# A second feed-forward computed by block products: gate, up and down in pairs of tiles

## The reference, cut to what matters

```python
D_MODEL, D_FF, SEQ, MACARON_WEIGHT = 1024, 2816, 512, 0.5

def swiglu(h, w_gate, w_up, w_down):
    return (jax.nn.silu(h @ w_gate) * (h @ w_up)) @ w_down

def ffn_sublayer(t, shift, scale, gate, norm_g, w_gate, w_up, w_down):
    h = modulate(rms_norm(t, norm_g), shift, scale)
    return t + gate * (MACARON_WEIGHT * swiglu(h, w_gate, w_up, w_down))
```

## Time and profile before

| what | us |
|---|---|
| median of 3 executions | 1463.39 (1462.80 to 1463.84) |
| profiled execution, first to last instruction | 1459.6 |
| TensorE busy in it | 1429.1 (98%) |
| VectorE / ScalarE / GpSimd busy | 705.8 / 265.9 / 664.1 |
| second feed-forward behind its first segment, on TensorE | 1150.2 to 1446.9 |

### The profile page before, as it was taken

One profiled execution on the slowest core, in us unless ns is written; L12 is line 12 of the kernel. 1 busy time (PEld: TensorE's weight loads), 2 busy tenths in 40 slices (PEclk: granted clock), 3 DMA queues, 4 the chain that ended last, 5 costly groups with the idle time before them and its releaser, 6 DMA issues.

```text
span 1459.6 us, 19101 instructions
## 1 busy us (share of the span) xinstructions
PE 1429.1 (98%) x7912; PEld 1250.1 (86%) x7912; DVE 705.8 (48%) x1032; ACT 265.9 (18%) x440; POOL 664.1 (46%) x389
## 2 busy tenths in 40 slices
PE   7999999999999999999999999999999999999997
PEld 3699999999999999987898888888898888888886
DVE  2774467467454554246636449625775112112114
ACT  3320010010010010023634321124131000000104
POOL 1363443433433433433610456624738557566661
PEclk9999999999999999999999999999999999999999
DMA  9532353353343343114310278384646323233321
GB/s 350 159 109 63 117 147 117 104 146 104 117 129 121 117 122 116 44 38 125 88 30 1 59 193 224 103 258 155 204 134 187 101 87 101 87 101 101 95 65 58
DMA packets 232563, 174.31 MB, mean 119 GB/s; under 512 B 28664, under 2 KB 212124, under 8 KB 232476
## 3 DMA queue, kind: packets, MB, share of 16 engines
q1 hardware_dynamic: 213296, 142.50, 33.4%
q10 hardware_dynamic: 19180, 30.58, 6.5%
HBM read 155.26 MB, written 17.79 MB: 119 GB/s over the span
## 4 chain that ended last, share of the span: by engine, by line
PE 93%; DVE 3%; ACT 1%; issue 1%; DMA 1%; POOL 0%; SPq 0%; DVEq 0%; POOLq 0%; ACTq 0%
PE ps L888 59%; PE ps L1143 15%; PE ps L1146 4%; PE ps L897 2%; PE ps L920 2%; PE ps L1240 2%; PE ps L1095 1%; PE ps L985 1%; PE ps L976 1%; PE ps L1393 1%; PE ps L1050 1%; PE ps L1347 1%; PE ps L1351 1%; PE ps L1162 1%; DMA x_in<-in_ctx_dram 1%
## 5 line engine op out<-in xcount | busy, mean ns | idle before, releaser
L818 POOL TENSOR_SCALAR w_hi<-w_raw 128x1024 fp32r<-128x1024 f32 (+1 forms) x187 | 211.6, 1131 | 745.2 <-issue 458.4
L821 POOL TENSOR_TENSOR w_lo<-w_raw,w_hi 128x1024 fp32r<-128x1024 f32 (+1 forms) x187 | 451.1, 2413 | 15.6
L888 PE MATMUL ps<-h_hi,w_lo 128*128 128x384 f32 (+1 forms) x1224 | 381.4, 360 | 0.0
L888 PE MATMUL ps<-h_hi,w_hi 128*128 128x384 f32 (+1 forms) x1224 | 378.6, 358 | 0.0
L888 PE MATMUL ps<-h_lo,w_hi 128*128 128x384 f32 (+1 forms) x1224 | 378.4, 358 | 0.0
L888 PEld LDWEIGHTS ps<-h_hi,w_lo 128*128 128x128 f32 x1224 | 221.9, 189 | 23.7 <-issue 2.5
L888 PEld LDWEIGHTS ps<-h_hi,w_hi 128*128 128x128 f32 x1224 | 223.9, 189 | 20.4
L888 PEld LDWEIGHTS ps<-h_lo,w_hi 128*128 128x128 f32 x1224 | 223.7, 189 | 20.4
L2196 DVE SCALAR_TENSOR_TENSOR ps<-ps,silu 128x768 f32<-128x768 f32 (+1 forms) x44 | 36.5, 831 | 254.6 <-PE ps L888 248.4
L2226 DVE SCALAR_TENSOR_TENSOR x<-ps,mod,x 128x512 f32<-128x512 f32 x88 | 64.8, 750 | 168.8 <-PE ps L1146 91.4
L1143 PE MATMUL ps<-act_hi,w_lo 128*128 128x512 f32 x336 | 133.7, 398 | 1.8 <-DVEq L2201 1.8
(11 more groups left out here) (374 smaller groups left out, 1868.4 us busy)
## 6 DMA issues: line engine op xcount, KB each, us to landing
w_raw<-in_ffn_w_gate_dram SPq DMA_DIRECT2D x44, 512.0 KB, 3.9
w_raw<-in_ffn_w_up_dram SPq DMA_DIRECT2D x44, 512.0 KB, 3.9
w_raw<-in_ffn_w_down_dram SPq DMA_DIRECT2D x40, 512.0 KB, 3.6
ada_w<-in_ada_w_dram ACTq DMA_DIRECT2D x32, 512.0 KB, 4.3
w_raw<-in_w_in_dram SPq DMA_DIRECT2D x32, 512.0 KB, 4.1
ada_w<-in_ada_w_dram SPq DMA_DIRECT2D x30, 512.0 KB, 4.8
c_scr<-cp ACTq DMA_DIRECT2D x16, 288.0 KB, 4.1
b_scr<-bt_sb ACTq DMA_DIRECT2D x16, 256.0 KB, 3.9
```

The source lines that it names most:

```text
L818: pool.tensor_scalar(w_hi[:, s, 0:cols], w_raw[:, s, 0:cols], 1.0, 1.0, ALU.mult, ALU.mult)\
L821: pool.tensor_tensor(w_lo[:, s, 0:cols], w_raw[:, s, 0:cols], w_hi[:, s, 0:cols].bitcast(F32), ALU.subtract).then_inc(w_split, 1)
L888: last = pe.matmul(mv[2], st, mv[part], start=(first and q == 0), stop=(n == len(terms) - 1 and q == 2))
```

## The change

The first segment stays. The other 18 hidden tiles are taken as nine pairs. Gate of a pair is a 1024x256 by 1024x512 product. It is cut into 2x2 blocks of weights and 2x2 blocks of `h`, and computed by Winograd's form of Strassen's scheme: seven block products in place of eight, each 4 x 3 matmuls of 256 columns. Up of the pair likewise. A "group" is the gate or the up of one pair. The order of stages is written out in `STAGES`: group 0, group 1, then for each pair the gate group, the down projection of the pair before, the up group; the last two down projections end it. So there are seven gate groups with a down projection behind them (groups 2, 4, ..., 14).

- **Sums of h** (`tiles_of_h`, `copy_h`, `tile_hi`): four sums of blocks of `h`, built once in the first segment in the odd PSUM banks, VectorE 28 operations of 128x512, ScalarE 12 copies. Each stands behind the ada additions of a hidden tile. TensorE waits for the first two (`t_ok`) before `ada_sums`.
- **Sums of weights** (`weight_sums`): four additions or subtractions of 128x512 on VectorE for each group, one operand or the result in PSUM banks 3 and 7, with block A21 first copied to bank 3 by ScalarE (`copy_a21`).
- **High and low parts**: high parts move from GpSimd to ScalarE (`prepare`), in blocks of 128x512 through eight half slots, seven blocks ahead (`LEAD`). GpSimd makes the low parts, but VectorE those of the two sums that lie in PSUM (`low_ahead`).
- **Partial products**: ScalarE copies three partial results of a group out of PSUM (`part`), VectorE adds them to later products in three additions of 128x256 (`quarter_ok`), then come SiLU, product, high copy and low part by quarters of 128x256.
- **Loads**: both units of a stage are loaded when GpSimd has made the low part of the last block of the stage two before (for a down stage, of its blocks one by one).
- **Semaphores**: two are gone, and the gate loads share those of the first ada tiles.

Its core, with the order of the queues:

```diff
@@ constants
+PAIRS = (FF // P - SEG) // 2
+HT = NL // 2
+HK = KD // 2
+PRODUCTS = ("p1", "p7", "p6", "p4", "p5", "p2", "p3")
+RAW_BLOCK = {"p1": (0, 0), "p4": (1, 1), "p2": (0, 1)}
+SUMS_FOR = {"p7": 1, "p6": 4, "p5": 4, "p3": 4}
+BY_DVE = ("p6", "p5")
+LEAD = 7
+STAGES = [("group", 0), ("group", 1)]
+for _m in range(1, PAIRS - 1):
+    STAGES += [("group", 2 * _m), ("down", _m - 1), ("group", 2 * _m + 1)]
+STAGES += [("group", 2 * PAIRS - 2), ("group", 2 * PAIRS - 1), ("down", PAIRS - 2), ("down", PAIRS - 1)]
@@ sync
+            def raw_read(st, v):
+                if st < 2:
+                    sp.wait_ge(w_split, PAIR_UNIT0 + 2 * st + v + 1)
+                elif STAGES[st - 2][0] == "group":
+                    pool_low_made(sp, BLOCK0[st - 2] + NPROD - 1)
+                else:
+                    pool_low_made(sp, BLOCK0[st - 2] + 2 * v + 1)
@@ tensor
                         if not two and nth == 0 and v == 2 * tiles - 1:
+                            pe.wait_ge(t_ok, 4)
                             pe.wait_ge(acc_ok, ada_added(ADA_MIX + 1, KD))
...
+            def group(q):
...
+                block_product(q, 0, "a", True, False)
...
+                block_product(q, 1, "b", True, False)
+                pe.wait_ge(part_ok, 3 * q + 1)
+                block_product(q, 2, "a", False, False)
+                pe.wait_ge(part_ok, 3 * q + 2)
+                block_product(q, 3, "b", False, True)
+                pe.wait_ge(part_ok, 3 * q + 3)
+                block_product(q, 4, "a", False, False)
...
+                block_product(q, 5, "c", True, True)
+                pe.wait_ge(quarter_ok, 3 * q + 2)
+                block_product(q, 6, "a", False, True)
@@ scalar
+            def copy_a21(q):
+                raw_here(act, stage_unit("group", q) + 1)
...
+                act.activation(ps[:, 3, :], raw_block(q, 1, 0), ACT.Copy).then_inc(a21_copied, 1)
+            def prepare(b):
...
+                if b + 2 in GROUP_AT:
+                    copy_a21(GROUP_AT[b + 2])
+            def group(q):
...
+                b = block_of("group", q, 0) + LEAD
+                for i in range(3):
+                    part(i, "aba"[i])
+                    prepare(b + i)
+                prepare(b + 3)
+                prepare(b + 4)
+                quarter(0)
+                prepare(b + 5)
+                quarter(1)
+                prepare(b + 6)
+                quarter(2)
+                quarter(3)
@@ vector
+            def weight_sums(q):
...
+                for f in range(2):
+                    raw_here(dve, stage_unit("group", q) + f)
+                dve.wait_ge(a21_copied, q + 1)
...
+                TT(s3, a11, a21, ALU.subtract).then_inc(sum_ok, 1)
+                TT(s1, a21, a22, ALU.add).then_inc(sum_ok, 1)
+                dve.wait_ge(sum_ok, 4 * q + 2)
+                TT(s2, s1, a11, ALU.subtract).then_inc(sum_ok, 1)
+                dve.wait_ge(sum_ok, 4 * q + 3)
+                TT(s4, a12, s2, ALU.subtract).then_inc(sum_ok, 1)
+            def st_group(q):
...
+                def event(i):
+                    b = block_of("group", q, i)
+                    sums_ahead(b + LEAD)
+                    low_ahead(b + LEAD - 1)
+                for i in range(3):
+                    event(i)
+                product_done(dve, q, 3)
+                dve.wait_ge(part_ok, 3 * q + 3)
+                TT(bank_b, bank_b, s2, ALU.add).then_inc(quarter_ok, 1)
+                event(3)
+                product_done(dve, q, 4)
...
+                TT(last_quarter(q), bank_a, s7, ALU.add).then_inc(quarter_ok, 1)
+                event(4)
+                if up:
+                    gated(0)
+                    gated(1)
+                product_done(dve, q, 5)
+                TT(bank_c, bank_c, s1, ALU.add).then_inc(quarter_ok, 1)
...
@@ vector, first segment, behind the ada additions of tile f_
+                            tiles_of_h(f_)
```

More of the change, by code:

```diff
@@ new lines, in bank_read @@
+            def bank_read(q, name):
+                if q < 2:
+                    for j in range(down_job(0, 0) - 4, down_job(0, 0)):
+                        if 2 * (j % 4) == 4 * q + "abc".index(name):
+                            was_read(pe, j)
+                    return
+                m = q // 2 - 1 - (q % 2 == 0 or q == GROUPS - 1)
+                for e, bank in enumerate(DOWN_BANKS[m] if m >= 0 else ()):
+                    if bank == 4 * (q % 2) + "abc".index(name) and bank not in DOWN_BANKS[m][e + 1:]:
+                        was_read(pe, down_job(m, e))
@@ L1499, in _ @@
+            for kind, n in STAGES:
+                (group if kind == "group" else down)(n)
             for k in range(4):
@@ L1624, in ada_tile, with ffn @@
                 act.dma_start(ada_w[:, s, :], ada_src(g, k)).then_inc(ada_here[s], 16)
-            def ffn(jobs, parts, n, act_base):
+            def ffn(jobs, parts, n, act_base, blocks_of_h=None):
                 def seg(part, i):
@@ L1922, in _, with copy_h, tile_hi @@
                 hi_half(1, k)
-            ffn(JOB["ffn2"], PARTS2, NL, FF // P)
+            def copy_h(n):
+                act.wait_ge(hb_ok, KD)
+                for b in range(2):
+                    act.activation(odd_bank(1 - n, b), two(h_hi[:, HK * n:HK * n + HK, HT:2 * HT], b).bitcast(F32), ACT.Copy)                        .then_inc(h_copied, 1)
+            def tile_hi(t):
+                for b in range(2):
+                    act.wait_ge(t_made, 2 * t + b + 1)
+                    act.activation(two(t_hi(T_ORDER[t]), b), odd_bank(T_BANKS[t], b), ACT.Copy).then_inc(t_hi_ok, 1)
@@ L1924, in _ @@
+            copy_a21(0)
+            for b in range(LEAD):
+                prepare(b)
+            for kind, n in STAGES:
+                if kind == "group":
+                    group(n)
+                else:
+                    for i in range(4):
+                        prepare(block_of("down", n, i) + LEAD)
             norm(3, JOB["norm3"], NL)
@@ new lines, in st_down @@
+            def st_down(m):
+                for e in range(KD):
+                    j = down_job(m, e)
+                    is_done(dve, j)
+                    STT(x[:, e, 0:NL], ps[:, DOWN_BANKS[m][e], :], mod[:, 64 + e, 0:1], x[:, e, 0:NL], ALU.mult, ALU.add)\
+                        .then_inc(slot_read[j % 4], 1)
+                    if m == PAIRS - 1 and e:
+                        add_square(3, e - 1, NL)
+                    if e % 2:
+                        b = block_of("down", m, e // 2)
+                        sums_ahead(b + LEAD)
+                        low_ahead(b + LEAD - 1)
+                if m == PAIRS - 1:
+                    add_square(3, KD - 1, NL)
+                was_read(dve, down_job(m, KD - 1))
@@ L2232, in seg @@
                             ada_add(ADA_START + nth, KD - 1)
+                        if q and k == 3:
+                            weight_sums(0)
+                        if q and k == 6:
+                            low_ahead(block_of("group", 0, 2))
                         if tiles == TAIL and k:
@@ L2716, in _ @@
             ffn(JOB["ffn2"], PARTS2, NL, 2, FF // P)
+            low_ahead(block_of("group", 0, 4))
+            weight_sums(1)
+            for kind, n in STAGES:
+                (st_group if kind == "group" else st_down)(n)
             was_read(dve, JOB["norm3"])
```

300 lines of the change are left out of this document (291 added, 9 removed).

## The result

| kernel | median us | executions | ratio to the kernel before |
|---|---|---|---|
| before, beside it | 1463.10 | 1461.41 to 1463.84 | |
| changed | 1483.16 | 1482.83 to 1488.62 | 1.0149 [1.0131, 1.0167] |
| changed, timed a second time | 1487.02 | 1485.74 to 1489.69 | 1.0156 [1.0143, 1.0170] |

What follows compares the result with a forecast made beforehand. The prediction took TensorE, busy for 98% of the span, as the bound. Its terms -14.4 - 2.8 + 7.2 + 19.6 = +9.6 us took the median 1463.39 to 1473.0 us, range 1453 to 1486.

Steps and rivals of the forecast that it cites:

- Part 1: Gate and up of the 18 later tiles: 1512 narrow matmuls in place of 864 wide ones, gain 14.4 us.
- Part 2: Five VectorE detours at segment ends go, as the down projection now runs one pair behind: gain 2.8 us.
- Part 3: First segment: VectorE's h sums delay TensorE, 5 us before the ada sums, 2 in the fourth down job; loss 7.2 us.
- Part 4: Seven gate groups before a down projection: TensorE waits 2.8 us each before the seventh product, loss 19.6 us.
- Edits costed at nothing: Partial-product copies, high and low parts, other groups' weight sums, and removed semaphores: no added time.
- The rival of the other side: Queues hide more: VectorE gets weight tiles early, h sums fit its idle time; 1458 or 1446 us; chance 0.24.

Runs made afterwards that it cites:

- filled waits: Changed kernel with TensorE making the sixth product three times over in the seven gate groups before a down projection; 1479.98 us, against 1487.02 unfilled beside it.
- short h sums: Changed kernel with the 20 additions and subtractions for the sums of h run over 8 of 256 columns per block; 1479.94 us, one execution.
- Short weight sums: Changed kernel with the weight sums of the groups from the third on run over 16 of 512 columns, order untouched; 1465.67 us, one execution.
- sums moved behind the addition: Changed kernel, with VectorE's four weight sums behind the addition for product 5 in the seven gate groups before a down projection; 1459.30 us, ratio 0.9965.
- both orders mended: Changed kernel with weight sums behind product 5's addition, second SiLU quarter earlier in those gate groups, and most h sums later in the first segment; 1451.67 us, ratio 0.9919.

## Why the prediction was wrong in size

The forecast's four parts, with what the runs showed:

| part | forecast | measured |
|---|---|---|
| 1. narrow matmuls | -14.4 | -14.4 (0.120 us apart, as said) |
| 2. waits at the ends of segments | -2.8 | -2.8 (no wait ahead of a down projection) |
| 3. first segment | +7.2 | +5.1 of waits |
| 4. seven gate groups | +19.6 | +22.7 (20.9 of waits, 1.8 of restarts) |
| TensorE at 1.2 GHz behind the waits | not in the sum | +11.2 (4.0 and 7.2) |
| sum | +9.6 | +21.8 (spans: +21.5) |

- **The step that failed** is in parts 3 and 4: each wait was costed at its own length, and TensorE was taken to go on at 0.2267 and 0.120 us a matmul behind it. In its place, the clock fell behind six of the eight waits, and the slow matmuls took 11.2 us more. Of the 4.0 in the first segment some 2.6 stand where TensorE would have waited for VectorE anyway (the slot at 1138.3, above), so about 1.4 + 7.2 = 8.6 us are net. They are most of the 12.2 us by which the sum was off; 3.1 are part 4's longer waits and restarts, 0.5 the rest of part 3. The filled waits show the pair part's share as an effect of the idle time, not of the work around it.
- **The trace of before had it.** The rows that the forecast rests on do not show it: TensorE's clock reads 1.00 through the earlier trace rows, where no wait is longer than 0.3 us. Elsewhere the same trace does. Behind a wait of 2.76 us at 53.46 the clock reads 0.58, and from 401.85 it reads 0.57 with no wait at all; ahead of that stand 32 matmuls of one column and 8 of 128 columns (397.32 to 401.9):

```profile
53.46:57.46 4.00, 4.00 (x14) 4.00 (x15) 4.00 (x9) 4.00 (x9) 0.00 (x0) 0.58 0.00 0
401.85:405.85 4.00, 4.00 (x15) 4.00 (x15) 2.87 (x5) 0.81 (x1) 2.70 (x2) 0.57 0.00 0
```

- **Part 1** held. The 109.2 ns that the forecast gives from the Trainium skill ("TensorE: Matmul & The Clock Gate", Back-to-back issue gap) did not show: neighbouring starts in the block products lie 0.12 us apart.
- **Part 2** held: the list of waits has none in front of the down projections of the pairs.
- **Part 3**, the first wait, was right (5 forecast, 5.83 measured), and the short h sums show that it is theirs. The second, 2 us in the fourth down job, did not show, because slow matmuls stood in its place: VectorE's low part came within 0.5 us of the forecast, but TensorE came later still. By the slot alone the loss would have been 7.7 us (9.1 less 1.4, an estimate), beside the 7.2 of the forecast. So VectorE's queue was worked out rightly. The 5.1 in the table is smaller because slow matmuls filled part of that time.
- **Part 4**, the mechanism was right in each link, and the chain of waits shows it. The second load took 5.27 us there, issued 0.41 us behind the first, against my 5.3 and 0.37; but it took 6.5 and 6.7 in two of the seven places, which makes their waits 3.8 and 4.0. The other five were 2.5 to 2.8. Short weight sums and sums moved behind the addition confirm both halves of the chain. The restart, 0.26 us each, was missing.
- **Edits costed at nothing** held: no wait in other groups.
- The rival of the other side named hidden waits for a fast kernel. Reordering does what the change alone did not: with both orders mended the kernel is 11.9 us faster than before, of the 17.2 that parts 1 and 2 offer. Of the missing 5.3, 2.9 lie in the first segment and 2.9 in the pair part, which has two waits of 1.4 and 1.1 us left; the tail is 0.7 shorter.

## What to carry to other kernels

When TensorE is busy for 98% of the span, a wait of two to six microseconds on it can cost more than its length: add a possible half-speed stretch behind it (here 1.4 us a fall in one profile and about 2.2 in another), and see the clock in windows of a few microseconds, for the page's slices and the busy share hide it. Look for such stretches anywhere in the trace of the kernel before, not only where the change will be. Before a cheaper algorithm is judged by its time, look at what stands in the helper engine's queue ahead of the one result that the main engine wants: here one call moved by one place was worth about 25 us, more than the algorithm saves. If a wait can't be removed, useless work in it can be worth its while.

## What the runs showed of the hardware

- **The clock can fall behind waits of a few microseconds in a busy stream.** In the second feed-forward it fell behind waits of 1.92, 2.18, most of those from 2.5 to 2.7, and all from 3.8 to 5.8 us; it did not fall behind waits of 0.3 to 1.5, 1.85 and 1.87 between block products or wide matmuls, nor behind others of 2.50 to 2.84.
- **It is in part chance.** Among the half-token jobs of the first segment TensorE waits 1.52 to 1.54 us for VectorE (released by `h_lo`) in every one of the eleven profiles, with the same work around it. The clock fell behind this wait in five of them and not in six. One of each kind, the kernel before and the version with the sums behind the addition:

```profile
1082.25:1086.25 4.00, 3.72 (x27) 3.31 (x28) 2.77 (x8) 1.28 (x3) 0.00 (x0) 1.00 0.45 131
...
1084.44:1088.44 4.00, 4.00 (x21) 4.00 (x22) 2.67 (x7) 1.01 (x2) 0.00 (x0) 0.57 0.44 131
```

  The 2.5 us wait near 660 us has a fall behind it in seven of the eleven, the 2.76 us wait near 53 us in all. What decides was not settled.
- **It also falls without a wait.** In the trace of before it fell with no wait ahead of it behind 32 matmuls of one column and 8 of 128 (shown above, at 401.85), and at 289.6 behind the same sequence. In the version with both orders mended it fell behind a wait of only 1.38 us and 16 matmuls of one column.
- **What a fall costs.** In the changed kernel's pair part 7.2 us for five falls; with short h sums about 11 for five, by the same account (313.6 less 279.3 of matmuls, 21.3 of waits and 1.8 of restarts); in the kernel before with waits put in, some eight wide matmuls 0.427 us apart behind 2.18 us, which is 1.6 us.
- At the lower clock 512 columns start 0.427 us apart and 256 columns 0.213 us. The Trainium skill ("TensorE: Matmul & The Clock Gate", section "Wait — 56ns, not 53.3ns?") gives N/1.2 GHz for this, 426.7 ns for 512, and the trace agrees. At the upper clock its 215.7 ns for 512 columns does not agree with the 226.7 of the earlier trace rows.
- The same page (section "A second HAM failure mode: psum-queue depth-cycling") says of a kernel that idles briefly and often between groups of matmuls that its clock swings between the two levels and that this costs throughput. These runs agree on the cost. They differ in what it took: single waits from 1.53 us on were enough, while the waits of 0.3 to 1 us showed no fall.
- Of two loads of 512 KB issued 0.41 us apart the first landed after 3.8 to 4.1 us (5.5 once) and the second after 5.2 to 5.5, in two places 6.5 and 6.7, where single ones took 3.9.
